# ScalarE's copy of the fourth turned pair, before or after the exponentials of the first pair

## The reference, cut to what matters

```
q, k, v = split(norm(h) @ w)            # w comes in units of 512 rows x 512 columns
z = q @ k.T * scale + bias              # blocks of 128 queries x 256 keys
p = exp(z - max(z)); p = p / sum(p)     # stick-breaking: p = exp(log sigmoid(z) + sum of log keeps)
o = p @ v
```

## Time and profile before

| | |
|---|---|
| median of 3 runs | 1100.59 us (1099.68 to 1101.82) |
| span of the profiled execution, first to last instruction | 1096.3 us |
| time of the profiled execution itself | not listed; the median lies 4.3 us above its span |
| TensorE busy | 1008.8 us (92%) |
| VectorE busy | 641.2 us (58%) |
| ScalarE busy | 599.4 us (55%) |
| mean granted TensorE clock | 0.976 |

### The profile page before, as it was taken

The page is one execution under the profiler, slowest core; times in us unless marked ns, Lnnn a source line. Parts: engine busy times, 40 slices in busy tenths (PEclk is TensorE's granted clock), DMA queues, the critical chain, the costliest instruction groups (busy, mean ns, idle before and its releaser), DMA issues.

```text
span 1096.3 us, 13515 instructions
## 1 busy us (share of the span) xinstructions
PE 1008.8 (92%) x5026; PEld 825.2 (75%) x5026; DVE 641.2 (58%) x811; ACT 599.4 (55%) x922; POOL 21.8 (2%) x21
## 2 busy tenths in 40 slices
PE   4977789999999998789999999899999998899998
PEld 3866567888887786577888887687787876788876
DVE  3357656655455546456555555767585665667654
ACT  5466545545445546445544545657566566765661
POOL 1000003000000000001000000000000000000000
PEclk8998899999999999899999999999999999999999
DMA  7422317555664453229566555354533433336550
GB/s 265 138 73 82 111 47 261 192 191 166 202 196 163 156 191 118 74 85 310 201 195 195 183 191 185 125 190 143 165 115 115 134 101 132 101 119 206 168 192 39
DMA packets 99405, 170.34 MB, mean 155 GB/s; under 512 B 3668, under 2 KB 52747, under 8 KB 99365
## 3 DMA queue, kind: packets, MB, share of 16 engines
q1 hardware_dynamic: 96704, 161.23, 44.4%
q0 software_dynamic: 2336, 8.47, 2.3%
q10 hardware_dynamic: 324, 0.10, 0.0%
HBM read 168.68 MB, written 1.11 MB: 155 GB/s over the span
## 4 chain that ended last, share of the span: by engine, by line
PE 83%; ACT 8%; DVE 6%; issue 2%; DMA 0%; ACTq 0%; DVEq 0%
PE acc L431 16%; PE acc L391 12%; PE acc L393 11%; PE acc L392 11%; PE pair_ps L393 7%; PE pair_ps L391 7%; PE pair_ps L392 7%; ACT logit L886 3%; PE turn_ps L505 2%; PE acc L482 2%; ACT w_hi L754 1%; PE turn_ps L449 1%; ACT uT_hi L785 1%; PE pair_ps L493 1%; PE pair_ps L492 1%
## 5 line engine op out<-in xcount | busy, mean ns | idle before, releaser
L1221 DVE TENSOR_TENSOR w_lo<-w_raw,w_hi 128x2048 fp32r<-128x2048 f32 (+3 forms) x156 | 351.5, 2256 | 165.1 <-ACT w_hi L754 165.0
L754 ACT ACTIVATE w_hi<-w_raw 128x2048 fp32r<-128x2048 f32 (+3 forms) x156 | 290.5, 1863 | 106.4 <-PE acc L393 61.2
L391 PE MATMUL acc<-w_hi,uT_hi 128*128 128x512 f32 (+3 forms) x564 | 224.6, 398 | 13.3 <-DVE w_lo L1221 6.4
L393 PE MATMUL acc<-w_hi,uT_lo 128*128 128x512 f32 (+3 forms) x564 | 217.7, 386 | 0.0
L392 PE MATMUL acc<-w_lo,uT_hi 128*128 128x512 f32 (+3 forms) x564 | 217.5, 386 | 0.0
L391 PEld LDWEIGHTS acc<-w_hi,uT_hi 128*128 128x128 f32 x564 | 107.9, 191 | 36.4 <-DVE w_lo L1221 9.2
L391 PE MATMUL pair_ps<-w_hi,uT_hi 128*128 128x512 f32 x320 | 126.5, 395 | 0.0
L393 PE MATMUL pair_ps<-w_hi,uT_lo 128*128 128x512 f32 x320 | 124.9, 390 | 0.0
L392 PE MATMUL pair_ps<-w_lo,uT_hi 128*128 128x512 f32 x320 | 124.6, 389 | 0.0
L393 PEld LDWEIGHTS acc<-w_hi,uT_lo 128*128 128x128 f32 x564 | 107.7, 191 | 21.3
L392 PEld LDWEIGHTS acc<-w_lo,uT_hi 128*128 128x128 f32 x564 | 108.1, 192 | 18.6
(11 more groups left out here) (207 smaller groups left out, 1121.0 us busy)
## 6 DMA issues: line engine op xcount, KB each, us to landing
w_raw<-in_w_in SPq DMA_DIRECT2D x50, 1024.0 KB
w_raw<-in_w_gate SPq DMA_DIRECT2D x44, 512.0 KB
w_raw<-in_w_up SPq DMA_DIRECT2D x44, 512.0 KB
w_raw<-in_w_down SPq DMA_DIRECT2D x22, 1024.0 KB
w_raw<-in_w_out SPq DMA_DIRECT2D x12, 1024.0 KB
w_raw<-in_w_qkv SPq DMA_DIRECT2D x12, 1024.0 KB
w_raw<-in_w_branch SPq DMA_DIRECT2D x6, 1024.0 KB
bias<-rel_rows POOLq DMA_DIRECT2D x5, 1024.0 KB, 10.3
```

Source lines behind the costliest of these rows:

```text
L391: mm(o, xh, wh[:, k, :], start=first and k == 0, stop=False)
L393: done = mm(o, xl, wh[:, k, :], start=False, stop=last and k == len(kts) - 1)
L754: activation(w_hi[:, slot, 0:width], w_raw[:, slot, 0:width], ACT.Copy).then_inc(hi_done, 1)
L1221: v.tensor_tensor(w_lo[:, slot, 0:width], w_raw[:, slot, 0:width], w_hi[:, slot, 0:width].bitcast(f32), ALU.subtract).then_inc(lo_done, 1)
```

## The change: where the fourth pair is copied

In step 1 of `project_and_attend`, ScalarE's stream copies pairs 1 and 2, then does what `attention_step` holds for that step (the exponentials of pair 0), and only then copies pair 3. The same instructions with the same waits are issued; two neighbouring parts of the stream are exchanged. No other engine's stream is changed.

```diff
-                    for t in ((0,), (1, 2, 3))[s] if s < 2 else ():
+                    for t in ((0,), (1, 2))[s] if s < 2 else ():
                         copy_pair(kind, t, pair0)
                     attention_step(kind, s, pair0, head0, kt0)
+                    if s == 1:
+                        copy_pair(kind, 3, pair0)
                     if kind == "sb":
                         if s % 2:
                             chunks[s // 2]()
```

## The result

The changed kernel takes 1084.28 us (median of 4 runs, 1081.88 to 1085.15), the kernel before 1100.32 us (4 runs, 1099.68 to 1101.82).

A forecast was written before the change was run, and what follows sets the result against it. It took TensorE's waits at line 505, a delay of order in ScalarE's stream, as the bound. 8.75 + 2.82 + 0.73 = 12.3 us off the 1096.3 us span, plus 4.3 around it, gave 1088.3 us, range 1085.8 to 1092.5.

The forecast's parts named there:

- What bounds the kernel, and the delay of order: TensorE, 92% busy, waits at line 505 for exponentials whose input was ready five microseconds earlier, behind copy 3 in ScalarE's stream.
- Third layer, 8.75 us: Five groups: exponentials move into ScalarE's idle 2.37 us, gaining 1.75 us each at line 505; bounds 0 and 9.05.
- Rival 1: Third layer: step 2's exponentials don't move, so 4.9 us of the gain is given back, making 1093.2 us; 12%.
- Banded group, 2.82 us: Line 505's whole wait for VectorE's division goes, 2.82 us, as the exponentials end earlier; bounds 1.75 and 2.82.
- Stick-breaking group, 0.73 us: The exponential fits before copy 3, so ScalarE's chunk copy and the chain behind start 0.73 us earlier; bounds 0 and 0.73.
- Weights and DMA, nothing: Units were loaded two steps before and the queues are asked nothing new, so weights and DMA were taken at nothing.
- rival 4: Copy 3 stands behind late maxima and comes 0.73 us later in seven groups, 5.1 us slower: 1105.7 us; 2%.
- rival 3: TensorE at line 505 is really held by something the exchange doesn't move, so time stays at 1100.6 us; 2%.
- The time around the span, 4.3 us: The runs' median lies 4.3 us above the profiled span; the same 4.3 was added to the new span.
- The clock, no gain: TensorE's removed waits of 1.81 us cost no clock, since the stretch after one shows 1.00, so none is given back.
- The rivals' clock case: TensorE: one slow clock restart more or fewer, 1.7 us either way, giving 1090.0 or 1086.6 us; 8%.
- the 12.3 us taken off the span: Whole kernel: 8.75 + 2.82 + 0.73 us off the span of 1096.3 us, giving 1084.0 us.

The follow-up runs named there:

- e2: Kernel before with the exchange in the third layer's five groups alone: 1089.95 us (4 runs), ratio 0.991 to the kernel before.
- e3: Kernel before with the exchange in the banded group alone: 1094.78 us (5 runs), ratio 0.9948 to the kernel before.
- e7: Kernel before, unchanged, run for a second profile: 1101.17 us, span 1099.4 us.
- e8: Kernel before, unchanged, run for a third profile: 1099.89 us, span 1098.1 us.
- e15: Kernel before, unchanged, run for a fourth profile: 1100.67 us, span 1098.9 us.
- e5: Kernel before, order kept, extra matmuls filling TensorE's waits at line 505 (11 banded, 7 in each third-layer group): 1096.08 us, ratio 0.9961.
- e9: Kernel before, order kept, with 11 extra matmuls in the banded group's wait alone: 1100.83 us (13 runs), ratio 1.0003.
- e10: Changed kernel with 12 extra matmuls in TensorE's 3.31 us wait ahead of the last group: 1083.23 us, ratio 0.9837 to the kernel before.
- e1: The changed kernel run again, all three kinds of group, against the kernel before: 1083.28 us (5 runs), ratio 0.9848.
- e11: Changed kernel with fills of 5 to 16 extra matmuls in TensorE's waits in `attend`: 1084.26 us (5 runs), ratio 0.9857 to the kernel before.
- e12: Changed kernel with extra matmuls both ahead of the last group and in `attend`'s waits: 1085.17 us (6 runs), ratio 0.9867 to the kernel before.

## Why the prediction was right, and where it was wrong

**What bounds the kernel, and the delay of order:** right. The exponentials ran where the idle time was.

**Third layer, 8.75 us:** right, 1.71 to 1.79 us a group, 8.8 in all, and e2's time agrees (8.4 to 11.6). In the last group the wait at unit 2's first matmul went from 0.36 to 0.51 us, the limit by ScalarE's chunk copy that the working named. Rival 1, the gain given back in step 2, is refuted by the 0.64 us that stayed.

**Banded group, 2.82 us:** right, 2.9 us in the aligned profiles and no wait left. As an expectation of e3's time it was too small by 2.8 us (1.5 to 4.2).

**Stick-breaking group, 0.73 us:** right; 0.63 us at line 505 and 0.73 by the next wait in the aligned profiles, too little for a run's time.

**Weights and DMA, nothing:** no new wait for a rounding or a load stands in the changed list of waits that answers to the exchanged copies.

**Slower (rival 4) and not what it says (rival 3):** refuted, the waits are gone, and copy 3 comes no later. That was closest in the stick-breaking group, and there it follows the turn of pair 3 by 0.63 us as before (67.42 to 68.05 then, 68.34 to 68.97 now).

**The time around the span, 4.3 us:** wrong in what it was, and its number held by luck. The step took the difference between a span and a median for an overhead. The overhead is 1.7 to 1.8 us; 2.6 us were the luck of the execution that was profiled. The new median lies 4.2 us above the new span (1084.28 less 1080.1), only because the execution profiled there was a quick one too. So this step is not the miss: all of it lies in the 12.3 us taken off the span, where 16.2 went.

**The clock, no gain:** this is the step that failed: "the removed waits of this length cost no clock, and their going gives none back". It put at nothing what measured some 4 us. It was read from one stretch, 742 to 747 us, at a clock of 1.00, of an execution in which none of the six waits was followed by the lower clock; behind that one wait e7, e8 and e15 don't show it either. In e7 and e8 three of the same six were, at 1.0 to 1.6 us each. The rivals' clock case had the price of one about right (1.7 us) and counted one stretch more or fewer; with six waits removed it had to count all that they bring on. e5 measures in one number what the idle waits cost beyond their length: 4.2 us (2.7 to 5.7) come from filling them and changing no order. That the exchange's excess is this same effect is argued from the size, and from e3, the one part whose excess is clear of noise; it isn't shown place by place. In the two profiles set against one another above none of the six waits is hit in either, and the excess lies where the lower clock fell otherwise, between 100 and 157 us and near 700. TensorE: Matmul & The Clock Gate, in the Trainium skill ("HAM oscillation"), whose rule the prediction set aside on this point, says that idle gaps between bursts send TensorE to the lower clock; the gaps in its example are longer than these six. The profiles agree with it in part: 0 to 3 of six gaps of 1.8 to 2.8 us were followed by the lower clock (0.57 to 0.72 granted in the stretches shown).

**What stays open.** In size the medians close: 12.4 of order and 4.2 of clock are 16.6 us, and 16 to 17 were measured. In part that is chance, since 1.6 of e5's gain lies ahead of the last group, where the changed kernel gained nothing. The share of each wait doesn't close. e9 brought nothing where e3, which removes the same wait, brought 2.8 us beyond it; e9's added waits lengthen the five others by 0.16 us, and whether that is why they were hit was not tried without them. And the two profiles of the changed kernel reach the banded group some 2.6 us earlier, beyond the 0.7 us of the exchange, than the profiles of before do on average, while e10's, with the same code up to there, does not. That is probably chance, since both are of quick executions at a mean granted clock of 0.98, where seven unprofiled ones have 0.973 or 0.974; the size is near that of the effect in dispute, and no usual execution of the changed kernel was profiled.

## What to carry to other kernels

Where an engine's stream holds a copy that waits for another engine in front of work whose input has long been ready, exchange them: the price is read from the idle time in front of the copy, and here it came out to within 0.1 us a group. Price a removed wait of TensorE at its length, and leave room above it for the lower clock that waits bring on: here about 4 us over six waits, one stretch costing 1.0 to 1.6 us. How often it comes is to be had from several profiles, never from one, and e9 shows that a fixed price per wait doesn't foretell a single one. Compare the profiled execution's own time with the median before taking anything from it as typical, in both kernels; the time around the span hardly varies (1.7 to 1.9 us here but for two executions), and what is left over is that execution's luck.

## What the runs showed of the hardware

One thing was not expected. VectorE's subtraction for `w_lo` takes 2.29 us by itself. Issued while GpSimd does its one 128x4096 addition, it ends only 2.15 us after GpSimd has ended, in every profile. VectorE's timeline of e1:

```profile
187.68 6.10 DVE L1223 TENSOR_TENSOR w_lo<-w_raw,w_hi 128x2048 fp32r<-128x2048 f32 x1 [0.20 <-ACT w_hi L754]
```

GpSimd's timeline of e1:

```profile
180.87 10.77 POOL L358 TENSOR_TENSOR bias<-bias,m_chunk 128x4096 f32<-128x4096 f32 x1 [9.39 <-DMA bias<-in_rel_band]
```

GpSimd ends at 191.64, the subtraction at 193.78: it had taken 6.10 us, 3.8 more than by itself. A subtraction issued before the addition is not held: in e1 the second of the pair ahead starts at 180.42, 0.45 us before GpSimd, and takes its 2.29 us. TensorE does not wait for the held one there. In e11 the addition, released by a DMA and not by the order of the kernel, comes 0.67 us before the second of that pair instead, which then takes 11.13 us. VectorE's timeline of e11:

```profile
179.96 13.34 DVE L1232 TENSOR_TENSOR w_lo<-w_raw,w_hi 128x2048 fp32r<-128x2048 f32 x2 [1.98 <-ACT w_hi L763]
...
193.23 0.86 DVE L1472 SCALAR_TENSOR_TENSOR qkv<-turn_ps,norms,qkv 128x256 f32<-128x256 f32 x2
```

GpSimd's of e11:

```profile
181.50 9.65 POOL L358 TENSOR_TENSOR bias<-bias,m_chunk 128x4096 f32<-128x4096 f32 x1 [8.27 <-DMA bias<-in_rel_band]
```

Those two take 4.49 us in e1 and 13.34 here, the attention behind them starts late, and 5.8 us are lost on TensorE's path between 188 and 199 us. They are most of the 7.0 us by which e11's profiled time of 1091.29 lies over its median of 1084.26. The other 16 profiles have the first order. e11's run of 1088.35 and e12's of 1087.7 to 1089.8 us are of a like size, but were not profiled.
